# Layer step on one core: operands of the first up-projection tiles

## The reference, cut to what matters

```python
def conv_ffn(h, rows, cols, w_up, w_dw, b_dw, w_down):
    up = h @ w_up                       # h: tokens x 1024, w_up: 1024 x 5632
    a, g = jnp.split(up, 2, axis=-1)    # two halves of 2816 features
    g = depthwise_3x3(g, w_dw) + b_dw   # on the 16 x 64 grid of the latent tokens
    return (jax.nn.gelu(g) * a) @ w_down

h = modulate(layer_norm(x), sh2, sc2)
x = layer_norm(ALPHA * x + g2 * conv_ffn(h, ...), ln2_g, ln2_b)
```

## Time and profile before

| | before |
|---|---|
| median of 3 runs | 1378.75 us (1377.24 to 1381.05) |
| the profiled execution, its own time | 1377.21 us |
| its span from first to last instruction | 1375.5 us |
| mean granted clock of TensorE | 0.969 |
| busy share PE / DVE / ACT / POOL | 93% / 75% / 43% / 49% |
| up projection, tile 1 and later | from 618.8 us of the span |

### The profile page before, as it was taken

One profiled execution on the slowest core, in us unless ns is written; L12 is line 12 of the kernel. 1 busy time (PEld: TensorE's weight loads), 2 busy tenths in 40 slices (PEclk: granted clock), 3 DMA queues, 4 the chain that ended last, 5 costly groups with the idle time before them and its releaser, 6 DMA issues.

```text
span 1375.5 us, 21762 instructions
## 1 busy us (share of the span) xinstructions
PE 1275.4 (93%) x7739; PEld 1178.4 (86%) x7739; DVE 1026.1 (75%) x1510; ACT 589.9 (43%) x1019; POOL 677.4 (49%) x507
## 2 busy tenths in 40 slices
PE   5899899988999699998799999999999999999994
PEld 3689899878988577898799999999999988888883
DVE  7565749674567688879977778877884789888588
ACT  5442123443335735444344444444453455345330
POOL 1001999333334131228869787888777874200001
PEclk9899999998999899999899999999999999999998
DMA  9433231363325253111353444445453579946692
GB/s 343 142 93 85 65 86 52 100 212 93 103 85 180 92 188 107 62 62 31 117 173 135 155 172 147 155 133 197 140 173 113 183 252 341 358 126 215 222 321 106
DMA packets 164339, 210.28 MB, mean 153 GB/s; under 512 B 10567, under 2 KB 101795, under 8 KB 164003
## 3 DMA queue, kind: packets, MB, share of 16 engines
q1 hardware_dynamic: 163774, 204.47, 45.4%
q0 software_dynamic: 288, 4.72, 0.9%
q10 hardware_dynamic: 197, 0.06, 0.0%
HBM read 161.49 MB, written 47.72 MB: 152 GB/s over the span
## 4 chain that ended last, share of the span: by engine, by line
PE 69%; DVE 15%; issue 5%; POOL 4%; DMA 4%; ACT 3%; SPq 0%; DVEq 0%; POOLq 0%; ACTq 0%
PE ps L1540 10%; PE ps L1538 10%; PE ps L1539 10%; PE ps L1194 10%; PE ps L1571 4%; PE ps L1572 4%; PE ps L1573 4%; DVE qk L2660 2%; DVE aacc L2678 2%; PE ps L1146 2%; DMA adaw<-in_w_ada 1%; PE ps L1105 1%; PE ps L1414 1%; PE ps L1416 1%; PE ps L1415 1%
## 5 line engine op out<-in xcount | busy, mean ns | idle before, releaser
L2972 DVE SCALAR_TENSOR_TENSOR ps<-gs,taps,ps 128x945 f32<-128x945 f32 (+2 forms) x176 | 215.8, 1226 | 56.5 <-ACT ps L1948 51.1
L1194 PE MATMUL ps<-h1hi,whi 128*128 128x384 f32 x432 | 155.1, 359 | 0.0
L1194 PE MATMUL ps<-h1lo,whi 128*128 128x384 f32 x432 | 147.6, 342 | 0.0
L1194 PE MATMUL ps<-h1hi,wlo 128*128 128x384 f32 x432 | 147.6, 342 | 0.0
L2313 POOL TENSOR_TENSOR rstd<-mv,neghalf 128x1 f32<-128x1 f32 x27 | 27.5, 1019 | 243.1 <-DVE mv L3146 165.3
L1571 PE MATMUL ps<-dwhi,uhi 128*128 128x512 f32 x290 | 113.1, 390 | 1.3 <-POOL dwlo L2165 1.3
L1573 PE MATMUL ps<-dwhi,ulo 128*128 128x512 f32 x290 | 112.9, 389 | 0.0
L1572 PE MATMUL ps<-dwlo,uhi 128*128 128x512 f32 x290 | 112.8, 389 | 0.0
L1538 PE MATMUL ps<-thi,xhi 128*128 128x288 f32 x320 | 95.4, 298 | 4.1 <-issue 4.1
L2165 POOL TENSOR_TENSOR wlo<-raw,whi 128x512 fp32r<-128x512 f32 x46 | 69.8, 1520 | 59.4 <-ACT whi L1643 29.1
L1538 PE MATMUL ps<-thi,whi 128*128 128x288 f32 x320 | 94.2, 294 | 2.0 <-POOL wlo L2165 2.0
(11 more groups left out here) (425 smaller groups left out, 3999.6 us busy)
## 6 DMA issues: line engine op xcount, KB each, us to landing
raw<-in_w_up SPq DMA_DIRECT2D x78, 256.0 KB, 4.5
u_rows<-val SPq DMA_DIRECT2D x22, 576.0 KB, 2.9
adaw<-in_w_ada SPq DMA_DIRECT2D x24, 512.0 KB, 4.0
st<-in_w_down SPq DMA_DIRECT2D x22, 512.0 KB, 4.3
t_rows<-st SPq DMA_DIRECT2D x11, 1024.0 KB, 5.0
raw<-in_w_in SPq DMA_DIRECT2D x40, 256.0 KB, 4.2
w_raw<-in_w_down SPq DMA_DIRECT2D x33, 256.0 KB, 5.2
v_raw<-u_rows SPq DMA_DIRECT2D x33, 256.0 KB, 4.9
```

The lines of the kernel that those rows point to most:

```text
L1194: last = mm(ps[:, bank, 0:GN], a[:, n % 2, k * P:(k + 1) * P], b[:, kk, grp(g)], start=(kk == 0 and a is whi and b is h1hi), stop=(kk == K ...
L2972: step(stt(a3[:, ro, co], g3[:, ri, ci], taps[:, tap:tap + 1], a3[:, ro, co], ALU.mult, ALU.add), 2 + m)
```

## The change

1. Tile 1's quarters go to ring places: `plain_slot(q)` gives xslot 2, 3, 1, 2 for q = 0 to 3, in place of 0, 1, 0, 1. ScalarE makes the high parts of quarters 0 and 1 once TensorE has done the output projection (pe_unit U_UP), ahead of the last `modulate2`, where before they came after the first copy out of PSUM. GpSimd makes all four low parts in a row.
2. All four t_lo are VectorE's, in the order of use 0, 1, 2, 3, each at another place in its queue: t_lo(0) ahead of conv(0), t_sum(3) behind conv(0), u_make(0), then t_lo(1), t_sum(2), t_lo(2), t_lo(3). TensorE's products wait on one semaphore for them.
3. ScalarE: gelu(0) stands ahead of the copy of tile 1's gate half and of t_hi(3) and the first s_hi; t_hi(2) moves into the first `seven`, behind s_hi of product 5; acc_init(1) ahead of the copy of the value half. The first body of ScalarE's loop is written out.
4. SyncE waits for t_ready 4 (t_sum(2) done) ahead of the loads of tile 3.

```diff
+        def plain_slot(q):
+            return xslot((2, 3, 1, 2)[q])
@@ SyncE
             load_st(0)
+            sp.wait_ge(t_ready, T_0 + 4)
@@ TensorE, plain_tile and seven
+                    hi_w, lo_w = plain_slot(q)
-                            for a, b in ((whi, h2hi), (whi, h2lo), (wlo, h2hi)):
+                            for n, (a, b) in enumerate(((hi_w, h2hi), (hi_w, h2lo), (lo_w, h2hi))):
-                    if n in (1, 2):
-                        pe.wait_ge(tlo_pool, L_0 + n)
-                    elif n in (4, 6):
-                        pe.wait_ge(tlo_dve, L_0 + 2)
+                    if n in (1, 2, 4, 6):
+                        pe.wait_ge(tlo_dve, L_0 + (1, 2, 4, 6).index(n) + 1)
@@ ScalarE, seven
                 s_hi(b, jj, 5)
+                if first_tile:
+                    t_hi(2)
                 formed(b, jj, 2)
@@ ScalarE, ahead of the loop
+            plain_hi(0, U_UP)
+            plain_hi(1, U_UP)
+            modulate2(NT - 1)
             act.wait_ge(pe_unit, U_UP + 2)
             fn(wide(gs[:, 0, :]), ps[:, 0:3, 0:GN], ACT.Copy).then_inc(g_out, 1)
             act.wait_ge(g_out, 1)
             acc_init(0, 0)
-            plain_hi(U_UP + 4, U_UP + 2)
-            plain_hi(U_UP + 5, U_UP + 2)
+            plain_hi(2, U_UP + 2)
             act.wait_ge(pe_unit, U_UP + 4)
             fn(wide(val[:, 0, :]), ps[:, 3:6, 0:GN], ACT.Copy).then_inc(val_copied, 1)
             t_hi(0)
             t_hi(1)
-            plain_hi(U_UP + 6, U_UP + 5)
-            t_hi(3)
-            plain_hi(U_UP + 7, U_UP + 6)
+            plain_hi(3, U_UP + 5)
+            gelu(0)
             act.wait_ge(pe_unit, U_UP + 6)
             fn(wide(gs[:, 1, :]), ps[:, 0:3, 0:GN], ACT.Copy).then_inc(g_out, 1)
+            t_hi(3)
+            s_hi(0, 0, 0)
             act.wait_ge(pe_unit, U_S - 1)
-            s_hi(0, 0, 0)
-            gelu(0)
+            s_hi(0, 0, 1)
+            act.wait_ge(g_out, 2)
+            acc_init(1, 1)
             act.wait_ge(pe_unit, U_S)
-            s_hi(0, 0, 1)
             fn(wide(val[:, 1, :]), ps[:, 3:6, 0:GN], ACT.Copy).then_inc(val_copied, 1)
             for n in range(2, 4):
                 s_hi(0, 0, n)
-            t_hi(2)
-            act.wait_ge(g_out, 2)
-            acc_init(1, 1)
-            with act.Fori(0, BODIES - 1) as b:
+            for jj in range(N_BODY):
+                seven(0, jj, split=jj % 2 == 1, first_tile=jj == 0)
+            with act.Fori(1, BODIES - 1) as b:
@@ GpSimd
-            lo(U_UP + 4)
-            lo(U_UP + 5)
-            t_lo(0)
-            lo(U_UP + 6)
-            lo(U_UP + 7)
-            t_lo(1)
+            for q in range(4):
+                plain_lo(q)
             ahead(0, 0)
@@ VectorE
             t_sum(0)
             t_sum(1)
-            t_sum(3)
+            t_lo(0, 2)
             conv(0, 0)
-            t_sum(2)
+            t_sum(3)
             u_make(0, 0)
             load_taps(1)
-            for q in (3, 2):
-                ...
+            t_lo(1, 3)
+            t_sum(2)
+            t_lo(2, 4)
+            t_lo(3, 3)
             dve.wait_ge(pe_unit, U_S)
```

More of the change, by code:

```diff
@@ L1502, in plain_tile @@
                             kk = (q % 2) * KT // 2 + k
-                            for a, b in ((whi, h2hi), (whi, h2lo), (wlo, h2hi)):
-                                last = mm(ps[:, 3 * (q // 2) + g, 0:GN], a[:, q % 2, k * P:(k + 1) * P], b[:, kk, grp(g)],
-                                          start=(kk == 0 and a is whi and b is h2hi), stop=(kk == KT - 1 and a is wlo))
+                            for n, (a, b) in enumerate(((hi_w, h2hi), (hi_w, h2lo), (lo_w, h2hi))):
+                                last = mm(ps[:, 3 * (q // 2) + g, 0:GN], a[:, k * P:(k + 1) * P], b[:, kk, grp(g)],
+                                          start=(kk == 0 and n == 0), stop=(kk == KT - 1 and n == 2))
                     last.then_inc(pe_unit, 1)
@@ L1929, in _ @@
                 norm2(t)
-            modulate2(NT - 1)
             def wide(x):
@@ L1948, in acc_init, with plain_hi @@
                 fn(acc_lat, gs[:, par, 0:LAT], ACT.Copy, scale=taps[:, 4:5]).then_inc(acc_begun, 1)
-            def plain_hi(n, free):
-                raw_wait(act, n)
+            def plain_hi(q, free):
+                raw_wait(act, U_UP + 4 + q)
                 act.wait_ge(pe_unit, free)
-                fn(whi[:, n % 2, :], raw[:, n % 4, :], ACT.Copy).then_inc(whi_ready, 1)
+                fn(plain_slot(q)[0], raw[:, q, :], ACT.Copy).then_inc(whi_ready, 1)
             def t_hi(q):
@@ L2037, in t_split, with seven @@
                 fn(st_r[:, 3, :], st[:, 2, :], ACT.Copy).then_inc(st_step, 1)
-            def seven(b, jj, end=False, aux=None, split=False):
+            def seven(b, jj, end=False, aux=None, split=False, first_tile=False):
                 j, par = N_BODY * b, jj % 2
@@ L2336, in _, with plain_lo @@
             pool.wait_ge(tb_ready, NT)
[L2338 to L2342, removed]
+            def plain_lo(q):
+                pool.wait_ge(whi_ready, U_UP + 4 + q + 1)
+                hi_w, lo_w = plain_slot(q)
+                sub_hi(lo_w, raw[:, q, :], hi_w).then_inc(wlo_pool, 1)
             def s_sum(b, jj, q):
@@ L3026, in _, with t_lo @@
             dve.wait_ge(h2lo_ready, NT)
+            def t_lo(q, formed):
+                dve.wait_ge(thi_ready, T_0 + T_ORDER.index(q) + 1)
+                dve.wait_ge(t_ready, T_0 + formed)
+                tt(tlo[:, q, :, :], tf[:, q, :, :], thi[:, q, :, :].bitcast(F32), ALU.subtract).then_inc(tlo_dve, 1)
             t_sum(0)
             t_sum(1)
+            t_lo(0, 2)
+            conv(0, 0)
             t_sum(3)
-            conv(0, 0)
-            t_sum(2)
             u_make(0, 0)
             load_taps(1)
-            for q in (3, 2):
-                dve.wait_ge(thi_ready, T_0 + T_ORDER.index(q) + 1)
-                tt(tlo[:, q, :, :], tf[:, q, :, :], thi[:, q, :, :].bitcast(F32), ALU.subtract).then_inc(tlo_dve, 1)
+            t_lo(1, 3)
+            t_sum(2)
+            t_lo(2, 4)
+            t_lo(3, 3)
             dve.wait_ge(pe_unit, U_S)
```

## The result

The changed kernel takes 1381.66 us (median of 16 runs; the kernel before 1377.18 over its 16 runs). The ratio is 1.0028, 95% interval 1.0017 to 1.0039, so it is slower by 3.9 us (2.3 to 5.4). One of the 16 runs took 6281.25 us, for a reason that nothing here shows; the ratio leaves it out, and the median of the other 15 is 1381.45. The profiled execution took 1378.70 us, 1376.9 of it span, mean granted clock 0.972.

A forecast was written before the change was run, and what follows sets the result against it. VectorE's queue bounds product 6: 5.1 us (t_lo(0), t_lo(1)) and 6.4 idle, less 4.8, 1.1 and 1.15, plus 0.6 rounding, give +5.1; 1378.75 + 5.1 = 1383.8 us. Own range 1381.5 to 1386.5; 8 in 10, 1377.5 to 1388.

The forecast's parts named there:

- one mechanism: VectorE's queue up to the addition behind conv(1) sets the start of product 6 of tile 2; sum +5.1 us.
- Tile 1: TensorE passes tile 1 without a gap, 144 matmuls in 25.0 us to 643.3, 8.0 us ahead of before.
- The early high parts: Two plain_hi of 0.6 us each between norm2 and the last modulate2 cost nothing, with 0.3 us to spare.
- VectorE's queue: Operations on VectorE, worked out step by step from t_sum(0) to conv(1) at 673.2; product 6 at 686.5, against 681.43.
- one turn: On VectorE, one GpSimd operation of 512 columns beside a sum adds 1.1 us to its 2.55.
- The idle time of 6.4 us: VectorE, done with t_sum(2) at 657.5, stands idle 6.4 us ahead of t_lo(2), waiting for ScalarE's t_hi(2).
- The stall ahead of product 0: TensorE, free at 643.3, waits until about 648.1 for GpSimd's low part; 4.8 of the 8.0 us are lost.
- SyncE's added wait: It holds tile 3's loads until 657.5, but the next wait, at 658.6, is later; taken at nothing.
- The written-out body: ScalarE's body replaces 1 of 4 loop rounds; its instruction fetching is bounded at 0 to 0.5 us.
- The low clock behind the long stall: TensorE's low clock after the wait ahead of product 6, some 12 us, may last less or longer: -0.7 to +0.8 us.
- (a): Rival: VectorE's idle time ahead of t_lo(2) does not arise; +0.8 us, -1 to +3, about 1379.6; chance 0.25.
- (b): Rival: tile 1's gain stays, VectorE free of turns and waits; product 6 at 675.4, -6.0 us, 1372.8; chance 0.1.

The follow-up runs named there:

- e1: Changed kernel with t_hi(2) on ScalarE moved ahead of s_hi of products 4 and 5; ratio to the kernel before 0.9997.
- e3: Changed kernel with t_hi(2) ahead of the first `seven` and ScalarE's first body back in its hardware loop; ratio to the kernel before 1.0005.
- e6: Changed kernel with s_hi of product 0 ahead of t_hi(3) on ScalarE; one execution, product 6 at 74.28 us from the first t_sum.
- e9: e8 with s_hi of product 0 also ahead of t_hi(3) on ScalarE; ratio to the kernel before 0.9955.
- e2: Kernel before with only tile 1's new ring places, early high parts and low parts in a row; ratio to the kernel before 0.9975.
- e8: Changed kernel with t_lo(0) and t_lo(3) on GpSimd, t_hi(2) ahead of product 4's s_hi, memsets in VectorE's wait for t_hi(2); ratio to the kernel before 0.9957.
- e7: Changed kernel with t_lo(0) back on GpSimd, beside conv(0); one execution, product 6 at 73.68 us from the first t_sum.

## Why the prediction was right, point by point

The forecast was slower by 5.1 us, by one mechanism; measured are 3.9 us by the ratio and 3.93 up to product 6 in the traces. The mechanism held at each step below, and the size came out 1.2 us too large. The measured 1381.66 is only just inside the forecast's own range, 1381.5 to 1386.5. The forecast time of 1383.8 lies 2.1 us above it: 1.2 of that is the sum, and 1.6 is that the kernel before has a median of 1377.18 over more runs, not the 1378.75 that the sum stood on; the other way go 0.6 by which the medians lie further apart (4.5) than the ratio says (3.9). The prediction had also called 4.1 us the least that a measurement can tell from no change, and gave 0.51 to more than that. The 3.9 lie under it, where it gave 0.37; the 16 runs of each kernel tell less than 4.1 us from nothing (2.3 to 5.4).

*Tile 1* went as worked out: no gap, 140 matmuls in a window of 24.00 us, and done 8.1 us sooner than before from the first t_sum, where 8.0 were forecast. The early high parts are hidden behind the wait for the transposes, with 0.47 us of it left.

*VectorE's queue.* Predicted and measured dates from the first t_sum: conv(0) done 27.5 and 27.4; t_sum(3) done 32.7 and 32.4; t_lo(1) done 37.0 and 36.4; t_sum(2) done 47.8 and 47.0; t_lo(2) started 54.2 and 53.4; conv(1) 63.5 and 62.45; product 6 76.8 and 75.64. The excess grows evenly, to 1.2 us. Some 0.5 of it is the term "one turn": I took 3.65 us for a sum with a turn of GpSimd, where three of them took 3.62, 3.52 and 3.50, and 7.2 for the pair of t_lo, which took 7.01. Another 0.3 is u_make(0) with the taps, taken at 1.7, from 642.4 to 644.1, and 1.39 in the rows. The rest is for the most part that I put durations end to end, while in the rows the next instruction often starts 0.08 us ahead of the end of the last (conv(0) at 625.32 against 622.84 + 2.56 = 625.40).

*The idle time of 6.4 us* was 6.35, at the place and for the reason given: both of its ends, t_sum(2) and t_hi(2), came 0.8 us sooner than forecast. e1 and e3 show that its part beyond t_hi(2)'s own length, 4.2 us, is the loss that the queue order on ScalarE makes.

*The stall ahead of product 0* was forecast at 4.8 and was 4.0 us; that it costs nothing in the end was a claim, and e1 (stall kept, loss gone), e6 and e9 bear it out.

*What was taken at nothing.* SyncE's added wait: its next loads started at 657.10, behind the third sum of GpSimd that ends at 656.91, as said, and e1 and e3 keep this wait and have no loss. The written-out body: nothing visible (e1 against e3); no run shows the 0.5 us that was its upper bound. The low clock behind the long stall: 20 matmuls in 4.60 us against 19 in 4.67 before, and 60 against 58 in the first 10 us, so a stall three times as long has cost no more of it.

*The rivals.* (a), the idle time not arising, is what e1 made: 71.84 for product 6 where the rival's working gave 72.5 (71.71 + 0.8). (b), the gain of tile 1 lasting, can't be had by itself: of 8 us e2 kept 2.5. The working behind (b), VectorE's own operations with neither turns nor waits, gave a product 6 six us ahead of before; e8 came to five, by moving work to where it costs nothing.

## What to carry to other kernels

When a stall on TensorE is removed, ask which date on another engine TensorE was waiting towards; if that engine's queue holds no gap up to the date, only what shortens that queue counts. An operation moved onto the full queue costs its length, and one put into an in-order queue behind waits that it doesn't need costs those waits: of the four t_his, one placed two s_hi too late was worth more than the whole tidy-up of tile 1 (3.8 against 2.5 us at product 6). On this pair of engines, lay GpSimd's work beside the VectorE instructions that read PSUM, and follow where it pushes what comes behind it.

## What the runs showed of the hardware that was not expected

The activation table load (the instruction that loads ScalarE's table for the gelu) ran ahead of the wait that the gelu has on the convolution: at 625.44, right behind the copy before it, for 1.28 us, while the gelu started at 636.18. I had put it behind the wait, 1.3 us too late, off the critical path. In the kernel before, the load ended at 647.18 and the gelu started at 647.20. The Trainium skill, "ScalarE: Activation LUTs", "What ACT_TABLE_LOAD costs", states about 1283 ns for the load and about 1380 for a drain beside it. The first agrees; of the second the rows show nothing on either side of the load: in the kernel before, the copy ahead of it ended at 645.88, the load began at 645.90, and the gelu followed 0.02 us behind its end.

In the changed kernel a turn of a GpSimd operation of 512 columns cost a VectorE sum 0.95 to 1.07 us (3.50 to 3.62 against 2.55), less than the operation's own 1.28. The Trainium skill, "SBUF — State Buffer", "Who interferes with whom", has it that a VectorE instruction with at most one SBUF input, outside the modes that use two ports, stays clear of GpSimd. e7 agrees over a GpSimd operation of 5.18 us: eight PSUM taps in 10.06 us.
